# Compressed keys behind each tile of the window keys in one product, and low query parts stored over the raw ones

## The reference, cut to what matters

```
s_c = einsum(qs, k_cmp) - slope * dist      # 63 compressed keys, padded to 64
s_s = einsum(qs, k_g)   - slope * dist      # "selected" branch: here all keys up to the query
s_w = einsum(qs, k_w)   - slope * dist      # "window" (local) branch: the last 512 keys
o   = gate0 * softmax(s_c) @ v_cmp + gate1 * softmax(s_s) @ v_g + gate2 * softmax(s_w) @ v_w
```

## Time and profile before

| | us |
|---|---|
| median of 3 runs | 1449.04 |
| lowest and highest | 1446.48 to 1452.92 |
| the profiled execution's own time | 1445.38 |
| its span, first to last instruction | 1443.7 |
| PE busy | 1410.8 (98%), 6733 matmuls |
| PE weight loads busy | 1163.2 (81%) |
| DVE busy | 1011.6 (70%) |
| ACT busy | 715.9 (50%) |
| POOL busy | 159.7 (11%) |

### The profile page before, as it was taken

How to read it: one execution, slowest core, us unless ns; L and a number is a source line. 1 busy time by engine, 2 the same in 40 slices (tenths; PEclk the granted TensorE clock), 3 DMA queues, 4 the chain that set the end, 5 groups by cost and what they waited for, 6 DMA issues and landing times.

```text
span 1443.7 us, 19186 instructions
## 1 busy us (share of the span) xinstructions
PE 1410.8 (98%) x6733; PEld 1163.2 (81%) x6733; DVE 1011.6 (70%) x2100; ACT 715.9 (50%) x1374; POOL 159.7 (11%) x176
## 2 busy tenths in 40 slices
PE   9999999999999999899999999999999999999997
PEld 7788787888878888678888778787888878787886
DVE  6254457888787888775558986859586877777654
ACT  6111136666666676632234564546454555555454
POOL 2000000010101001000050012020303030212100
PEclk9999999999999999999999999999999999999999
DMA  6363441122221222275233247381919273645653
GB/s 207 111 195 117 117 136 40 59 63 59 62 60 41 63 59 63 76 236 184 84 101 96 63 77 138 79 155 53 174 38 167 66 147 87 130 97 103 123 161 117
DMA packets 159532, 151.74 MB, mean 105 GB/s; under 512 B 12259, under 2 KB 124439, under 8 KB 159440
## 3 DMA queue, kind: packets, MB, share of 16 engines
q1 hardware_dynamic: 143312, 121.20, 27.6%
q0 software_dynamic: 16128, 29.37, 13.8%
HBM read 94.43 MB, written 56.10 MB: 104 GB/s over the span
## 4 chain that ended last, share of the span: by engine, by line
PE 88%; DVE 7%; issue 2%; ACT 2%; DMA 1%; DVEq 0%; POOL 0%; POOLq 0%; ACTq 0%; SPq 0%
PE psU L1865 7%; PE psU L1866 7%; PE psU L1867 7%; PE psX L2081 4%; PE psU L2271 4%; PE psU L2234 4%; PE psU L2235 4%; PE psU L2236 4%; PE psU L2272 4%; PE psU L2273 4%; PE psX L1865 3%; PE psX L1867 3%; PE psX L1866 3%; PE psX L2234 3%; PE psX L2235 3%; PE psX L2236 3%
## 5 line engine op out<-in xcount | busy, mean ns | idle before, releaser
L1591 DVE TENSOR_TENSOR ring_lo<-raw,ring_hi 128x512 fp32r<-128x512 f32 x150 | 103.3, 689 | 72.8 <-ACT ring_hi L1089 72.8
L858 POOL DMA_DIRECT2D residual_scratch<-csum x112 | 98.1, 911 | 493.1 <-DVE csum L1768 423.2
L1865 PE MATMUL psU<-ahi,whi 128*128 128x512 f32 x352 | 138.8, 394 | 0.2 <-DVE alo L1288 0.2
L993 ACT ACTIVATE pth<-psX 128x512 fp32r<-128x512 f32 x148 | 88.2, 596 | 99.1 <-PE psX L2081 98.7
L1867 PE MATMUL psU<-ahi,wlo 128*128 128x512 f32 x352 | 137.2, 390 | 0.0
L1866 PE MATMUL psU<-alo,whi 128*128 128x512 f32 x352 | 137.2, 390 | 0.0
L985 ACT ACTIVATE prob<-prob,nb 128x64 f32<-128x64 f32 (+8 forms) x192 | 114.8, 599 | 24.1 <-DVE nb L1479 23.2
L1089 ACT ACTIVATE ring_hi<-raw 128x512 fp32r<-128x512 f32 x150 | 92.7, 624 | 63.7 <-PE psU L2273 23.3
L1503 DVE TENSOR_TENSOR ptl<-psX,pth 128x512 fp32r<-128x512 f32 x132 | 90.6, 688 | 31.1 <-ACT pth L993 30.5
L1865 PE MATMUL psX<-ahi,whi 128*128 128x512 f32 x256 | 109.4, 427 | 1.2 <-ACT zst L1007 1.1
L1867 PE MATMUL psX<-ahi,wlo 128*128 128x512 f32 x256 | 100.6, 393 | 0.0
(11 more groups left out here) (328 smaller groups left out, 3763.8 us busy)
## 6 DMA issues: line engine op xcount, KB each, us to landing
raw<-in_w_ff_dram SPq DMA_DIRECT2D x120, 256.0 KB, 4.3
residual_scratch<-csum POOLq DMA_DIRECT2D x112, 256.0 KB, 5.9
wraw<-in_w_in_dram SPq DMA_DIRECT2D x31, 512.0 KB, 4.0
gate_scratch<-zst SPq DMA_DIRECT2D x32, 256.0 KB, 3.2
mg<-gate_scratch SPq DMA_DIRECT2D x16, 512.0 KB, 3.4
proj_scratch<-stage SPq DMA_DIRECT2D x15, 512.0 KB, 3.0
xt<-in_x_dram SPq DMA_DIRECT2D x8, 512.0 KB, 7.5
qraw<-proj_scratch SPq DMA_DIRECT2D x32, 128.0 KB, 2.9
```

The costliest lines, as they stand in the source:

```text
L858: pool.dma_start(resid[rows, cols], sums[b][e][:], accum_op=ALU.add).then_inc(added[b][e], 16)
L1591: nc.vector.tensor_tensor(lo, raw_of(g), hi.bitcast(f32), ALU.subtract).then_inc(w_lo, 1)
L1865: nc.tensor.matmul(ps, whi[:, slot, w], hi[:, k, cols], start=start, stop=False)
```

## The change

The window keys `kW` were one row of 1024 columns per group. They become 8 tiles of 192 columns: 128 window keys, and behind them a copy of the 64 compressed keys. So the last window tile of a query block and the compressed keys stand side by side, and one product (with its `ql` partner) makes both. The window tiles before the last one go in one product of up to 512 columns whose columns come in runs of 128, 192 apart. With four window tiles (i = 3) all four go together, and the compressed keys alone behind them.

ACT makes the eight copies (`spread_compressed`) at step n = 12, and PE waits for them (`kc_rows`) ahead of the first scores. The kW key copies write and read the 128-column runs.

The raw queries lose their own place: `qraw` now lies where `ql` lies, and DVE subtracts in place. The load of the queries for iteration it now waits until the scores of iteration it - 2 are done (`s_win`). Four small tiles of the setup move into the place of `vW`, which is not yet written then.

```diff
@@ places @@
         kS = place("kS", [P, GROUPS, S], f32r)
-        kW = place("kW", [P, GROUPS, S], f32r)
+        WC = P + CP
+        kW = place("kW", [P, GROUPS, TT, WC], f32r)
...
         QUERIES = cursor[0]
-        qraw = place("qraw", [P, 2, GR, P])
+        ql = place("ql", [P, 2, GR, P], f32r)
         qh = place("qh", [P, 2, GR, P], f32r)
-        ql = place("ql", [P, 2, GR, P], f32r)
...
+        cursor[0] = QUERIES
+        qraw = place("qraw", [P, 2, GR, P])
...
@@ SP @@
             def load_q(it):
                 g, i = ITER[it]
                 if it >= 2:
-                    sp.wait_ge(q_lo, it - 1)
+                    sp.wait_ge(s_win, GR * (it - 1))
@@ ACT @@
+            def spread_compressed():
+                act.wait_ge(misc_ev, M_CMP)
+                for t in range(TT):
+                    nc.scalar.activation(kW[:, :, t, P:WC], kC[:].bitcast(f32), ACT.Copy).then_inc(kc_rows, 1)
...
                 if n == 12:
+                    spread_compressed()
                     act.wait_ge(gate_sum, 1)
                     nc.scalar.activation(gate_t[:], gate_t[:], ACT.Tanh, scale=0.5).then_inc(gate_tanh, 1)
...
                 if n == 13:
-                    key_hi(kW, ldA, kw_in)
+                    key_hi(kW[:, :, :, 0:P], ldA[:].rearrange("p g (t c) -> p g t c", t=TT), kw_in)
@@ DVE @@
                 if n == 13:
-                    key_lo(1, kW, ldA)
+                    key_lo(1, kW[HD:P, :, :, 0:P], ldA[HD:P].rearrange("p g (t c) -> p g t c", t=TT))
@@ PE, scores @@
                 if e >= 1:
                     pe.wait_ge(m_win, e)
-                for c in range(0, w, HALF):
-                    n = min(HALF, w - c)
-                    ks = kW[:, g, a - w + c:a - w + c + n]
-                    nc.tensor.matmul(psS1[:, c:c + n], qh[:, s, r], ks, start=True, stop=False)
-                    nc.tensor.matmul(psS1[:, c:c + n], ql[:, s, r], ks, start=False, stop=True)
-                nc.tensor.matmul(psS1[:, w:w + CP], qh[:, s, r], kC[:, g], start=True, stop=False)
-                nc.tensor.matmul(psS1[:, w:w + CP], ql[:, s, r], kC[:, g], start=False, stop=True).then_inc(s_win, 1)
+                nt = w // P
+                whole = nt if nt == HALF // P else nt - 1
+                if whole:
+                    out, ks = psS1[:, 0:whole * P], kW[:, g, i + 1 - nt:i + 1 - nt + whole, 0:P]
+                    nc.tensor.matmul(out, qh[:, s, r], ks, start=True, stop=False)
+                    nc.tensor.matmul(out, ql[:, s, r], ks, start=False, stop=True)
+                out, ks = psS1[:, whole * P:w + CP], kW[:, g, i, (whole - nt + 1) * P:WC]
+                nc.tensor.matmul(out, qh[:, s, r], ks, start=True, stop=False)
+                nc.tensor.matmul(out, ql[:, s, r], ks, start=False, stop=True).then_inc(s_win, 1)
...
             pe.wait_ge(k_ready, 2)
+            pe.wait_ge(kc_rows, TT)
```

More of the change, by code:

```diff
@@ L132, in hybrid_trunk @@
         kS = place("kS", [P, GROUPS, S], f32r)
-        kW = place("kW", [P, GROUPS, S], f32r)
+        WC = P + CP
+        kW = place("kW", [P, GROUPS, TT, WC], f32r)
         vS = place("vS", [P, TT, GROUPS, 2 * HD], f32r)
+        V_WINDOW = cursor[0]
         vW = place("vW", [P, TT, GROUPS, 2 * HD], f32r)
@@ L180, in hybrid_trunk @@
         cw1 = place("cw1", [P, 2, CSTRIDE // 2, 2, HD])
+        assert cursor[0] <= STAGE
+        cursor[0] = V_WINDOW
         cw2 = place("cw2", [HD, 2, 2 * HD])
@@ L184, in hybrid_trunk @@
         chid2 = place("chid2", [HD, GROUPS, 2, CP])
-        assert cursor[0] <= STAGE
+        assert cursor[0] <= V_WINDOW + size_of([P, TT, GROUPS, 2 * HD])
         cursor[0] = STAGE
@@ L323, in hybrid_trunk @@
         half_b, gelu_arg, gelu_tanh = sem("half_b"), sem("gelu_arg"), sem("gelu_tanh")
-        k_ready = sem("k_ready")
+        k_ready, kc_rows = sem("k_ready"), sem("kc_rows")
         q_in = [sem("q_in0"), sem("q_in1")]
@@ L943, in key_hi @@
                 act.wait_ge(s, 32)
-                nc.scalar.activation(dst[:], src[:], ACT.Copy).then_inc(k_hi, 1)
+                nc.scalar.activation(dst, src, ACT.Copy).then_inc(k_hi, 1)
+            def spread_compressed():
+                act.wait_ge(misc_ev, M_CMP)
+                for t in range(TT):
+                    nc.scalar.activation(kW[:, :, t, P:WC], kC[:].bitcast(f32), ACT.Copy).then_inc(kc_rows, 1)
             def query_hi(it):
@@ L969, in _ @@
                     value_hi(M_VS + 1, vS, 1)
-                    key_hi(kS, ldB, ks_in)
+                    key_hi(kS[:], ldB[:], ks_in)
                 if n == 12:
+                    spread_compressed()
                     act.wait_ge(gate_sum, 1)
@@ L1356, in key_lo @@
                 dve.wait_ge(k_hi, b + 1)
-                nc.vector.tensor_tensor(dst[HD:P], src[HD:P], dst[HD:P].bitcast(f32), ALU.subtract).then_inc(k_ready, 1)
+                nc.vector.tensor_tensor(dst, src, dst.bitcast(f32), ALU.subtract).then_inc(k_ready, 1)
             n2 = GROUPS * NCMP
@@ L1440, in _ @@
                     value_lo(vS, 1, 2)
-                    key_lo(0, kS, ldB)
+                    key_lo(0, kS[HD:P], ldB[HD:P])
                 if n == 12:
```

## The result

The changed kernel takes 1439.93 us (median of 8 runs), the kernel before 1448.57 us (median of 8): 8.6 us less. The ratio is 0.9944, with a 95% interval of 0.9933 to 0.9955, that is 6.5 to 9.7 us less. The forecast was 1441.9 us and 7.1 us less. A second set of 5 runs beside the experiments gave 1439.94 us and a ratio of 0.9938 (0.9925 to 0.9951).

The account below looks back on a forecast made before the run. PE, with 88% of the chain that ended last (DVE 7%), was taken as the bound. Raw 9.6 us less 0.57, 1.32 and 0.64 gave 7.1, all else 0: 1449.0 - 7.1 = 1441.9 us, range 1436 to 1449.

Parts of the forecast that it names:

- 1) The raw gain: Scoring calls: 80 products fewer at 0.11 us give 8.8 us, cheaper products at tile 2 give 0.8; 9.6 us in all.
- 2) What DVE takes back: PE's waits for DVE in attention: minus 0.57 at tile 6, 1.32 at tile 7, 0.64 at tiles 2 and 0.
- about 2 us longer: Sign of being right: PE's waits in attention for DVE's last scaling (L1495) grow by this much in total.
- 3) to 6) The rest at nothing: Eight ACT copies, key copies in runs, in-place low query parts and reads through gaps: each taken as 0 us.
- All of it counts: Rival: in attention DVE's chains ride along with PE, so the full 9.6 us is saved, 1439.4 us; 15%.
- DVE takes back more: Rival: short iterations before tiles 7, 6, 5 and 4 give nothing; 2 to 4 us saved, 1446 us; 17%.
- The gapped read: Rival: long kW products read through gaps get slower, up to 18.6 us more if each run counts alone, 1460.5 us; 4%.
- it does not do what it says: Rival: a 192-column product takes as long as the 128 and 64 it replaces, 0.22 us; no change, 1449 us; 4%.

Follow-up runs that it names:

- e4: The kernel before with each pair of 64-column products on the compressed keys made twice, 128 more matmuls; 1459.63 us, ratio 1.0075.
- e5: The changed kernel with its layout, but products merged for query tiles 4 and 5 alone; 1444.61 us, ratio 0.9980.
- e6: The changed kernel with its layout, but products merged for query tiles 6 and 7 alone; 1445.71 us, ratio 0.9977.
- e7: The kernel before with DVE's scaling of the selected branch's probabilities left out at query tiles 6 and 7; 1444.08 us in one run.
- e8: The changed kernel with DVE's scaling of the selected branch's probabilities left out at query tiles 6 and 7; 1434.79 us in one run.
- e1: The changed kernel run again without an edit, for a second trace; 1439.94 us, ratio 0.9938.
- e2: The kernel before with only the in-place low query parts, the later query load and the moved setup tiles, products as before; 1448.38 us, ratio 0.9997.
- e3: The changed kernel with its key layout, gaps, copies and waits, but the products apart as before; 1448.58 us, ratio 0.9998.
- e10: The changed kernel with two blocks of gate products moved in front of PE's wait for DVE's last scaling, in seven iterations; 1440.05 us, ratio 0.9937.
- e9: The changed kernel with tile 4's selected scores split 320 and 320 and tile 1's window part made one pair of 384 columns; 1439.47 us, ratio 0.9931.

## Why the prediction was right

**1) The raw gain.** The pace of short products was right: loads stand 0.11 us apart in the earlier trace rows, in the changed kernel, and in e4. What a removed product gives back was taken too high. In the rest of attention, PE's time outside its waits, e5 and e6 have 3.2 and 3.1 us less for 32 products, 0.10 each and not 0.11; the whole merging has 389.52 - 381.31 = 8.2 us less between e7 and e8, two traces without a low stretch in attention. For e1 it comes to 8.1 to 8.5, an estimate: 7.09, the 1.05 by which its waits grew, and up to 0.35 more of waits that the dip may have covered (e6 has a wait of 0.32 us inside that stretch, e1 has none). So the raw gain was 8.1 to 8.5 us and not 9.6. A scoring call shows where a part goes: the first short product's load is made beside the long one before it (at 207.81 in the kernel before), so the four short products took 0.36 us (208.03 to 208.39) and not 0.44. The two of now take 0.20 (209.30 to 209.50). The page "TensorE: Matmul & The Clock Gate" of the Trainium skill, section "Back-to-back issue gap", has 81 ns for products of 128 columns, which would have made it 6.5 + 0.8 = 7.3 us, an estimate; the loads in the rows shown are 110 ns apart, and the 0.10 us found for a removed product lies between the page's figure and the one taken.

**2) What DVE takes back.** Each stretch from the second head's scores of a tile to those of the next, before less changed, against the terms of the forecast (a first head's 0.22 falls into the stretch before its tile):

| tile, group 0 | forecast | found | tile, group 1 | forecast | found |
|---|---|---|---|---|---|
| 7 | 0.22 | 0.28 | 7 | 0.00 | 0.14 (e6) |
| 1 | 0.22 | 0.21 | 1 | 0.22 | 0.30 |
| 6 | 0.44 | 0.32 | 6 | 0.31 | 0.36 |
| 2 | 0.52 | 0.53 | 2 | 0.52 | 0.54 |
| 5 | 0.66 | 0.63 | 5 | 0.66 | 0.61 |
| 3 | 0.22 | 0.22 | 3 | 0.22 | 0.20 |
| 4 | 0.66 | 0.64 | 4 | 0.66 | 0.66 |
| 0 | 0.88 | 0.82 | 0 | 0.66 | 0.63 |

The sums are 7.07 and 7.09, but that they agree so well is luck: the raw gain was 1.1 to 1.5 us smaller than forecast, and the loss was smaller by about as much (PE's waits grew by 1.1 to 1.4 us, forecast was 2.5). Two terms were too large, and their errors cancelled. The forecast "about 2 us longer" for the waits on L1495 missed for the same reason (0.9). The mechanism holds in kind tile by tile: full value at tiles 5 and 4 (there PE's waits even shrank a little, by 0.3 us in e5), less at the two others. With 0.20 a call four calls are worth 0.8 us; tile 7 kept 0.28 and 0.34 of it, tile 6 0.52 and 0.56 (its first call's part counted in). At tile 7 the loss was forecast at 0.66 each time and is nearer 0.5. At tile 7 the first 0.2 us shorten DVE's wait for PE, which was 1.52 us at the second head and is 1.34 now; at tile 6 the idle of 0.66 at 270.91 has become 0.35, and PE's wait of 1.23 is 1.53. DVE's timeline, twice, then PE's:

```profile
212.74 1.23 DVE L1481 CUSTOM_DVE_ANT_0 prob<-psU,T 128x1024 f32<-128x1024 f32 x1 [1.34 <-PE psU L2073]
...
271.38 1.09 DVE L1481 CUSTOM_DVE_ANT_0 prob<-psU,T 128x896 f32<-128x896 f32 x1 [0.35 <-PE psU L2073]
```

```profile
278.19 0.66 PE L2094 MATMUL psX<-ident,prob 128*128 128x128 f32 x4 [1.53 <-DVE prob L1506]
```

**3) to 6) The rest at nothing.** e2 and e3 show 0 for the in-place low parts and for layout and gaps. For the setup ahead of attention, which both leave partly open, e8 and e10 show it: they have the changed layout and no low stretch there, and their first scoring products start at 206.68 and 206.72 us, against 206.67 before. The eight copies took 1.70 us (0.3 each was forecast, 0.21 found) and came out of ACT's idle, 4.60 us for 6.19:

```profile
178.48 1.70 ACT L954 ACTIVATE kW<-kC 128x128 fp32r<-128x128 f32 x8
...
184.78 0.36 ACT L984 ACTIVATE gate_t<-gate_t 128x192 f32<-128x192 f32 x1 [4.60 <-DVE gate_t L1458]
...
197.21 1.92 ACT L949 ACTIVATE kW<-ldA 128x2048 fp32r<-128x2048 f32 x1 [6.05 <-DMA ldA<-proj_scratch]
```

The key copy in runs takes the same 1.92 us, and DVE's low part the same 2.29. The prediction's ground for this does not hold as it was read: 1.07 us for 1024 elements is 1.04 ns each and 1.92 for 2048 is 0.94, so the copies in runs of 64 did cost more per element. The zero was right all the same.

**The rivals.** "All of it counts" fell by the waits that grew and by e6; its 9.6 us was too high besides, since the raw gain itself was 8.1 to 8.5. "DVE takes back more" fell by e5 and the table. The gapped read fell by e3, and "it does not do what it says" by e4. By the medians alone (interval 6.5 to 9.7 us) "all of it counts" would not be out; the traces decide.

**What is left.** Attention explains 7.1 us. The medians say 8.6; 7.1 lies inside the first interval (6.5 to 9.7) and on the edge of the second (7.1 to 10.9). Behind attention, to the end of the span, the changed kernel took 1438.2 - 603.72 = 834.5 us, the kernel before 1443.7 - 608.46 = 835.2 and e3 1447.3 - 611.75 = 835.6. In those stretches PE's waits for DMA and for DVE's mixing (L1566) come and go by a microsecond from trace to trace (e5 has 1.0 and 1.7, e6 1.1 and 2.5). Over all traces the seven kernels with merged products take 834.5 to 836.4 us there and the five without 835.2 to 836.7, so the two groups overlap. Whether the change helps there or a few traces happened to differ is not settled.

## What to carry to other kernels

In this kernel a short product in a chain of load and multiply costs its weight load, not its columns (0.11 us to the next one at 64 as at 192 columns, 0.10 back when it goes): look for columns that share the stationary operand and lay them side by side, even at the price of copies of the moving operand. Before booking the saving, go tile by tile to the wait that follows it, and ask which instruction of the other engine's chain starts it: the saving counts only as far as that start moves. Check the terms one by one in the trace, even when the sum comes out. And work put in front of a wait needs its own inputs and its own PSUM bank free at that moment, and is missed where it stood before.

## What the runs showed of the hardware

- The scatter between executions goes with the clock: of the executions of the kernel before, beside the experiments, the seven with a mean granted clock of 0.997 or 0.998 took 1446.3 to 1448.8 us, the six with 0.992 to 0.994 took 1447.9 to 1452.5. In the traces, e3's first scoring product starts at 209.84 us, that of the kernel before at 206.67, with the same work ahead of it; in between there is a stretch at the low level in e3 (109 to 117 us, 0.61 and 0.54), which in the trace before is at 1.00. The changed kernel has a shorter one there (0.77 and 0.81 over 110 to 118) and starts at 207.94. e3, the windows:

```profile
109.00:113.00 4.00, 4.00 (x23) 3.90 (x23) 0.30 (x2) 0.57 (x2) 0.00 (x0) 0.61 0.91 264
113.00:117.00 4.00, 4.00 (x12) 3.08 (x11) 3.90 (x4) 0.55 (x1) 0.00 (x0) 0.54 0.61 129
```

- The same wait of 2.2 us was followed by a low stretch in e1 and e9 and not in e6. In e6:

```profile
424.00:432.00 8.00, 5.48 (x33) 4.43 (x32) 6.29 (x21) 5.97 (x15) 0.00 (x0) 1.00 0.27 83
```

- A moving operand in runs of 128 columns, 192 apart, costs nothing that can be seen (e3: 0.12 us for 256 gaps, with a scatter of 0.3).
- A gain and a loss on a waiting path are not mirror images: at the first tile 7 two loads fewer per head brought 0.28 us, two more cost 0.75 (e4), where PE's waits fell by 0.47.
